# Two attention blocks in one program: the second mixer's lists, halves and engines rearranged

## The reference

```
first_block:  h = rms_norm(x); proj = h @ w_in
              MoBA heads (8) and forgetting heads (8), causal, 64 wide
              merged = gate0 * (o_a @ w_branch_moba) + gate1 * (o_b @ w_branch_fox)
              x = x + merged @ w_out;  x = x + ffn(rms_norm(x))        (conv, silu, product)
second_block: p = rmsnorm(x) @ w_in_2, split into hq, hf, hi, hg, sq, sk, sv, iq, ik, iw, mq
  hgrn2:  b = cumsum(log f);  A[t,s] = sum_k q[t,k] exp(b[t,k]-b[s,k]) k[s,k],  s <= t
          o = A @ v + carried state;   o = rmsnorm(o) * silu(g)       (4 heads, 128 wide)
  dsa:    score = sum_h iw[h] relu(iq[h] . ik); keep the 64 best keys of each query;
          softmax attention over them                                 (4 heads, 64 wide)
  mem:    softmax attention over 256 memory tokens                    (4 heads, 64 wide)
          x = x + concat(o_hg, o_sa, o_mem) @ w_out_2;  x = x + ffn(rmsnorm(x))
```

## Time and profile before

| | us |
|---|---|
| median of 3 runs | 847.26 |
| the profiled execution | 844.03 |
| its span | 842.2 |
| TensorE busy | 779.6 |
| VectorE busy | 543.4 |
| ScalarE busy | 469.4 |
| GpSimd busy | 86.4 |

### The profile page before, as it was taken

How to read it: one execution, slowest core, us unless ns; L and a number is a source line. 1 busy time by engine, 2 the same in 40 slices (tenths; PEclk the granted TensorE clock), 3 DMA queues, 4 the chain that set the end, 5 groups by cost and what they waited for, 6 DMA issues and landing times.

```text
span 842.2 us, 10581 instructions
## 1 busy us (share of the span) xinstructions
PE 779.6 (93%) x3775; PEld 637.5 (76%) x3775; DVE 543.4 (65%) x799; ACT 469.4 (56%) x724; POOL 86.4 (10%) x52
## 2 busy tenths in 40 slices
PE   7998889997999999999999798787869999999998
PEld 4886769985788888888887676565646888888886
DVE  4777765858368777775555569887673776665640
ACT  3756577783267877773545735352543776666430
POOL 0023000000000000000000156543231000000000
PEclk6999989999999999999999899897679999999999
DMA  8668353535067554565565433311001766554730
GB/s 276 211 194 267 104 142 130 184 109 174 25 222 235 179 179 162 197 200 175 161 215 167 125 100 101 100 50 51 25 26 51 236 224 199 181 176 176 247 134 25
DMA packets 70986, 129.14 MB, mean 153 GB/s; under 512 B 5576, under 2 KB 17824, under 8 KB 70817
## 3 DMA queue, kind: packets, MB, share of 16 engines
q1 hardware_dynamic: 70366, 125.91, 46.1%
q10 hardware_dynamic: 578, 2.69, 0.9%
HBM read 127.54 MB, written 1.05 MB: 153 GB/s over the span
## 4 chain that ended last, share of the span: by engine, by line
PE 74%; DVE 13%; ACT 8%; issue 2%; DMA 2%; POOL 1%; ACTq 0%; DVEq 0%; POOLq 0%
PE acc L486 21%; PE acc L488 21%; PE acc L487 21%; DVE b_wlo L1376 3%; PE banks L805 2%; ACT b_whi L939 1%; PE banks L818 1%; PE banks L629 1%; PE banks L503 1%; PE banks L549 1%; DVE b_ss L1447 1%; DVE b_qraw L1454 1%; DVE b_qraw L1461 1%; POOL b_rp L1929 1%; DVE b_spare L1777 1%
## 5 line engine op out<-in xcount | busy, mean ns | idle before, releaser
L1376 DVE TENSOR_TENSOR b_wlo<-b_raw,b_whi 128x1024 fp32r<-128x1024 f32 (+4 forms) x222 | 252.9, 1179 | 101.8 <-ACT b_whi L939 100.7
L939 ACT ACTIVATE b_whi<-b_raw 128x1024 fp32r<-128x1024 f32 (+4 forms) x244 | 235.2, 1002 | 77.8 <-PE acc L488 22.4
L486 PE MATMUL acc<-b_whi,b_hhi 128*128 128x512 f32 (+4 forms) x528 | 204.7, 388 | 8.4 <-DVE b_hlo L1750 4.7
L487 PE MATMUL acc<-b_whi,b_hlo 128*128 128x512 f32 (+4 forms) x528 | 198.2, 375 | 0.0
L488 PE MATMUL acc<-b_wlo,b_hhi 128*128 128x512 f32 (+4 forms) x528 | 198.0, 375 | 0.0
L486 PEld LDWEIGHTS acc<-b_whi,b_hhi 128*128 128x128 f32 x528 | 101.0, 191 | 28.6 <-DVE b_hlo L1750 5.2
L486 PE MATMUL acc<-b_whi,b_ohi 128*128 128x512 f32 (+1 forms) x272 | 107.4, 395 | 6.5 <-DVE b_wlo L1376 2.9
L487 PEld LDWEIGHTS acc<-b_whi,b_hlo 128*128 128x128 f32 x528 | 101.1, 191 | 16.0 <-issue 1.5
L488 PEld LDWEIGHTS acc<-b_wlo,b_hhi 128*128 128x128 f32 x528 | 100.8, 191 | 15.8
L487 PE MATMUL acc<-b_whi,b_olo 128*128 128x512 f32 (+1 forms) x272 | 104.5, 384 | 0.0
L488 PE MATMUL acc<-b_wlo,b_ohi 128*128 128x512 f32 (+1 forms) x272 | 104.4, 384 | 0.0
(11 more groups left out here) (247 smaller groups left out, 866.6 us busy)
## 6 DMA issues: line engine op xcount, KB each, us to landing
b_raw<-in_w_in SPq DMA_DIRECT2D x48, 512.0 KB, 4.6
b_raw<-in_w_ffn_up SPq DMA_DIRECT2D x40, 512.0 KB, 4.7
b_raw<-in_w_ffn_in SPq DMA_DIRECT2D x40, 512.0 KB, 4.6
b_raw<-in_w_ffn_down SPq DMA_DIRECT2D x22, 512.0 KB, 5.5
b_raw<-in_w_ffn_out SPq DMA_DIRECT2D x22, 512.0 KB, 4.4
b_raw<-in_w_out SPq DMA_DIRECT2D x16, 512.0 KB, 3.7
b_raw<-in_w_in SPq DMA_DIRECT2D x12, 412.0 KB, 4.3
b_raw<-in_w_in SPq DMA_DIRECT2D x8, 410.0 KB, 4.5
```

The lines of the kernel that those rows point to most:

```text
L486: nc.tensor.matmul(o, a, wh, start=first, stop=False)
L487: nc.tensor.matmul(o, b, wh, start=False, stop=False)
L939: A(whi[:, n % SPLIT, 0:c["nk"], 0:c["n"]], raw[:, n % RAW, 0:c["nk"], 0:c["n"]], ACT.Copy)\
L1376: V.tensor_tensor(wlo[:, n % SPLIT, 0:c["nk"], 0:c["n"]], raw[:, n % RAW, 0:c["nk"], 0:c["n"]], whi[:, n % SPLIT, 0:c["nk"], 0:c["n"]].bit ...
```

## The change

In the first mixer `("sums", "kb")` stands one place later, after `scores 1`. The merge is taken apart: VectorE alternates gating and L1750, the banks are waited for tile by tile, and `wo1_0` and `wo1_1` are streamed in turns. In the second mixer GpSimd has nothing left to do: its subtractions and `kd`, `kx` go to VectorE. The decay products take a rounded table and `logf` in two rounded parts. Pairs are computed only inside halves of 64 tokens (plus one 64 x 64 block across), so that one bank holds them; ScalarE places the result (`place`). Heads and index heads run two at a time. Group order and number of large products stay.

```diff
+            stream("wo1_0", "wo1_1")
+        elif n != "hf":
+            stream(n, part=1)            # second mixer's groups; the list names both parts together
-        FIRST = {0: [("sums", "qb")]}
+        FIRST = {0: [("sums", "qb")], 1: [("sums", "kb")]}
-        LAST = {0: [("sums", "kb")], 1: [("sums", "fg0")], ...
+        LAST = {1: [("sums", "fg0")], ...

+            merged_T(0); gemm("wo1_0", 0, norm="merged"); merged_T(1); gemm("wo1_1", 0)
+            gemm("wo1_0", 1, norm="merged")
+            gemm("wo1_1", 1, between=lambda: norm_T("ffn1", 0), between_at=1)

+            merge(0, 0)                  # VectorE: L1741 and L1746 of one tile
+            merge(0, 1)
+            merged_lo(0, 0)              # VectorE: L1750 of one tile
+            merge(1, 0)
+            merged_lo(0, 1)
+            merge(1, 1)
+            lo_to(groups["wo1_0"]["at"][1] + 1 * PART)
+            for t in range(T):
+                merged_lo(1, t)
+            norm("ffn1", "wo1_0", "wo1_1", ohi, olo, gain_at(2), PART, PART)

+        MIX2 = [... *parts("iqb")[2:], ("pairs", 0), ("place", 0), ("decay", 1), ("sums", "iqb"), ...
+                *parts("sqk")[:2], ("pairs", 4), ("place", 4), ("decay", 5), ("turn", "mq"), ("best", 0), ("best", 1),
+                ("scores", 8), *parts("sqk")[2:], ("divide", 8), ("pairs", 5), ("place", 5), ("probs", 8), ("decay", 6),
+                ("best", 2), ("pv", 8), ("best", 3), ("sums", "sqk"),
+                *parts("hg")[:2], ("hout", 2), ("pairs", 6), ("place", 6), ("scores", 9), ("divide", 9), ("probs", 9), ("decay", 7),
+                ("best", 4), ("best", 5), ("pv", 9), ("turn", "sqk"),
+                *parts("hg")[2:], ("pairs", 7), ("place", 7), ("hout", 3),
+                ("sums", "hg"), ("best", 6), ("best", 7), ("chosen", 0), ("hgrn norm", 0), ("log", "g"), ("scores", 10),
+                ("exp", "g"), ("gemm", "wo2_0", 0), ("gemm", "wo2_1", 0), ("divide", 10), ("hgrn norm", 1), ("probs", 10),
+                ("scores", 11), ("divide", 11), ("pv", 10), ("gain", 0), ("out", 0), ("out", 2), ("probs", 11),
+                ("gemm", "wo2_0", 1), ("pv", 11), ("gemm", "wo2_1", 1), ("gemm", "wo2_0", 2), ("gemm", "wo2_1", 2)]

# decay, TensorE
-                    full(nc.tensor.matmul(X[b][:, :], logf[...], hgc[:, c:c + 512], ...
+                    nc.tensor.matmul(X[b][:, :], lfhi[...], table, start=True, stop=False)      # rounded parts
+                    full(nc.tensor.matmul(X[b][:, :], lflo[...], table, start=False, stop=True), ...
# ScalarE, once each
+            done(A(hgr[:, C_HC:C_HC + 9 * P], hgc[:, C_HC:C_HC + 9 * P], ACT.Copy), "hgrn table", "0")
+                    done(A(lfhi[:, :, :], logf[:, :, :], ACT.Copy), "log f hi", "0")            # ahead of ("exp", "k")
# VectorE, once
+                    done(V.tensor_tensor(lflo[...], logf[...], lfhi[...].bitcast(F32), ALU.subtract), "log f split", "0")
# pairs, TensorE
+                for n in range(1, LEVELS + 1):
+                    for r in range(2):   # own: 64 rows of the bank and 64 tokens
+                        nc.tensor.matmul(X[2][own, (n - 1) * 64:n * 64], k, q, start=True, stop=True)
+                full(nc.tensor.matmul(X[2][0:64, LEVELS * 64:512], kd[:, 0, 0:64], qd[:, 0, 64:P], ...
# VectorE, unit u
+                V.tensor_tensor(qd[:, :, :], dec[...], q..., ALU.mult)
+                V.tensor_tensor(kd[:, :, :], dec[...], k..., ALU.mult)
+                (kx for even u, qx for odd u)
+                done(V.tensor_tensor(masked[:, :], X[2][:, 0:448], hgc[:, C_HM:C_HM + 448], ALU.mult), "pairs masked", ...
+                done(V.tensor_reduce(near[:, u % 2, :], masked (448 elements to 64), AX.X, ALU.add), "weights summed", ...
# ScalarE, unit u: "pairs" copies the 64 x 64 block across; "place", which the list puts before "decay u + 1":
+                    act.wait_ge(*at("weights summed", f"{n}"))
+                    A(AT[0:64, t, 0:64], near[0:64, t, :], ACT.Copy)
+                    done(A(AT[64:P, t, 64:P], near[64:P, t, :], ACT.Copy), "weights placed", f"{n}")
# ScalarE, "out": new wait
+                    act.wait_ge(*at("bank3 full", "probs 11"))
# VectorE, every ("gemm", ...) of the second mixer; GpSimd's loop is gone
-                    lo_to(min(part_end(n, *rest) + 3 * PART, MIX2_LOW[0] - 1))
+                    lo_to(part_end(n, *rest) + 3 * PART)
```

More of the change, by code:

```diff
@@ L462, in full, with gemm @@
                 done(ins, f"bank{bank} full", step, i)
[L464 removed]
+            def gemm(name, c=None, i=0, norm=None, between=None, between_at=0):
                 g = groups[name]
@@ L581, in pair_pv, with mixed_scores @@
                 full(mm, 2, f"pv {g}")
-            def attn_scores(j):
-                q, k, _, whole = head(j)
-                b = j % 2
-                claim(b, f"scores {j}")
-                for start, steps in ((16, ("sqk",)), (20, ("mq", "mk"))):
-                    if j == start:
+            def mixed_scores(g):
+                for i in range(2):
+                    claim(i, f"scores {g}")
+                for start, steps in ((10, ("sqk",)), (8, ("mq", "mk"))):
+                    if g == start:
@@ new lines, in mixed_divide @@
+            def mixed_divide(g):
+                two = slice(first_head(g), first_head(g) + 2)
+                for i in range(2):
+                    dve.wait_ge(*(at(f"bank{i} free", f"scores {g}") if whole(g) else at("exps ready", f"{g}")))
+                done(V.reciprocal(rc[:, two, :], sm[:, two, :]), "sum inverted", f"{g}")
+                dve.wait_ge(*at("sum inverted", f"{g}"))
+                for i in range(2):
+                    pr, j = pair_probs(g, i), first_head(g) + i
+                    for t, c0, n in pair_parts(g):
+                        ins = V.tensor_scalar(pr[:, c0:c0 + n], pr[:, c0:c0 + n], rc[:, j, t:t + 1], None, ALU.mult)
+                done(ins, "probs ready", f"{g}")
```

551 lines of the change are left out of this document (267 added, 284 removed).

## The result

The changed kernel took 840.75 us (median of 20 runs, 836.67 to 844.19), the kernel before 846.16 beside it (20 runs, 839.47 to 853.22): ratio 0.9938, 95% interval 0.9918 to 0.9958, so 5.3 us faster where 15 were forecast. The time lies at the upper end of the forecast's own range of 825 to 841, with about a third of the forecast gain. The profiled execution took 841.02 us, with a span of 839.2.

What follows compares the result with a forecast made beforehand. Second mixer taken as bound by ScalarE at its start, then TensorE, and VectorE's queue from 508 us; merge 4.1, keys 0 and second mixer 10.8 sum to 14.9 us off the 847.3 median: 832 us, range 825 to 841.

Steps and rivals of the forecast that it cites:

- Merge, 4.1 us forecast: End of the first mixer: shorter TensorE waits around the merged transposes gain 4.1 us net, bounds 6 gained to 1 lost.
- about 0.7 us may be lost on the next norm's second half: Norm behind the merge: interleaving leaves one chunk of cover for four VectorE instructions, so about 0.7 us lost.
- Keys, 0: First mixer, step moved past `scores 1`: only queue order changes, so 0, between 3 us gained and 2 lost.
- Second mixer, 10.8 forecast: Whole second mixer, 444 to 649 us: 10.8 us ahead at its end.
- Net 6.0 us: Second mixer, 533 to 604 us, VectorE's queue: 20.2 us of work gone less what is added, 6.0 us gained.
- 1.0 back: Second mixer, 604 to 649 us: 3.8 us saved against 4.8 of longer chain, so 1.0 us given back.
- The `place` waits beyond those there now 0.4: Second mixer, 533 to 604 us: extra waiting because `place` precedes the next unit's exponentials on ScalarE, 0.4 us added.
- 0.4 where two heads' exponentials (4 x 0.47) plus a rounding of 1.05 stand between maximum and subtraction: Second mixer, 533 to 604 us: ScalarE's work for a head pair makes VectorE wait, 0.4 us added.
- (b): Rival, slots from `sqk` to `wo2`: subtractions and `place` waits run serially, so 4 us slower, 851; chance 0.13.
- (a): Rival, second mixer: shorter VectorE-ScalarE chain halves gaps after 531 us and clock losses, 11 us more, 821; chance 0.19.
- (c): Rival, no change: freed VectorE time goes back into long gaps at low clock, only the merge stays, 845; chance 0.14.
- (d): Rival, second mixer's pairs: small tiles 0.5 us a unit slower, not 0.6 faster, 835; counted within the forecast's 0.54.

Runs made afterwards that it cites:

- b1: Kernel before with GpSimd's second-mixer work (22 subtractions, the decayed keys) moved to VectorE and nothing else of the change: 841.6 us.
- e1: Changed kernel with the end of its first mixer (merge, order of the two output groups, leads of the subtractions) as before: 841.9 us.
- e2: Changed kernel with the leads of the subtractions around the merge given back, the rest of the new merge kept: 835.7 us.
- c1: Changed kernel with e2, e4 and e5 joined, and ScalarE's copy of mq's transposes ahead of unit 4's placing: 826.9 us.
- c2: c1 with pair 9's scores one step earlier on all engines, its division and the rounds of the eight largest moved to suit on VectorE: 827.5 us.
- c3: c1 with more moves in VectorE's list alone (maxima, divisions and masks of several pairs and units put earlier): 816.1 us.
- e6: Changed kernel with the norm of kb back in its old place, one step earlier in all engines' lists: 842.5 us.
- e5: Changed kernel with ScalarE's list alone altered: for units 0 to 4 the next decay's exponentials ahead of the copies placing the present unit's weights: 837.3 us.
- e4: Changed kernel with the late second-mixer lists of VectorE and ScalarE reordered, TensorE's list and all operations unchanged: 832.9 us.
- e7: Changed kernel with the second mixer's subtractions back on GpSimd, the decayed keys left on VectorE: 845.9 us.
- e10: Changed kernel with each unit's mask product and sum over levels done twice on VectorE: time up by 14.2 us.

## Why the prediction was wrong

The direction was right, the size a third.

**Merge, 4.1 us forecast: mis-sized.** Measured 0.1 to 1.7 (44.9 against 45.0, 46.2, b1's 45.2 and e1's 46.6). The two waits fell as drawn (1.07 and 0.30; 0.9 and 0.6 were forecast). The step that failed is "about 0.7 us may be lost on the next norm's second half": 3.75 us of wait more, and behind it 14 products of 256 columns 0.21 us apart instead of 0.12. It counted VectorE's instructions between two products and not the loads that wait for its subtractions. With the leads kept the stage takes 40.0 to 40.7 us (e2, c1, c2, c3), 5 under before.

**Keys, 0: within its bounds.** The wait is 0.7 us shorter; e6 is 1.8 us above the changed kernel by the medians and 3 by the ratios, at the edge of what the intervals tell apart.

**Second mixer, 10.8 forecast: 1.5 to 5.2 measured**, by which profile of before one takes. The milestones came true as far as 525.73 us, where sqk's first products start (532.53 before; counted from the stage's start 9.0 us ahead, 9.7 forecast). At the first product of wo2_0, at 604.02 before and at 598.29 now, it is 8.0 us ahead (2.3 against the second profile of before), where 11.8 were forecast, and at the end 5.2 (1.5), where 10.8 were. Durations and busy times were right nearly throughout: `qd` and `kd` at 1.09, sums at 0.93 (0.88), masks 0.62, gain products 0.69, pairs 1.15 (1.3), decays 1.2 (0.92), VectorE 121.8 (123). What failed is the term for 533 to 604, "Net 6.0 us", which took TensorE no further ahead, and the one for 604 to 649, "1.0 back", with 2.7 back (0.8 by the second profile). In them it is the steps that translate work into time. "The `place` waits beyond those there now 0.4": unit 4's mask and placing hold decay 5's exponentials, and bank 0, for 5.20 us, and e5 gets 3.8 back. "0.4 where two heads' exponentials (4 x 0.47) plus a rounding of 1.05 stand between maximum and subtraction": with the heads in pairs the chain of maxima, exponentials and division stood behind subtractions, masks, norms and rounds of the eight largest in VectorE's queue, and the waits around it are of 10.4, 11.0 and 4.8 us (with that order changed e4 gets 8.0 back, c3 23). Gaps of the first two's size were foreseen ("three or four gaps of 8 to 10 us"), but "not fewer microseconds of idle than now" left open how many more. It was 17, and the prediction's own mark for its failure, 45 us in all, is passed with 53. b1 shows the error from the other side: what the stage gained is, as closely as these runs tell, the relief of GpSimd.

**The rivals.** (b) is false as a whole: its subtractions in VectorE's queue pay (e7), though two of them stand in the wait of 10.37 us. (a), shorter chains, needed the other order (c3 goes beyond its 821). (c) is nearest in its mechanism, freed time given back in long waits at the low clock, but the merge, which it kept, stayed away too. (d) is false: the small tiles take 0.65 us less a unit. "TensorEngine Tiling (Array Packing)" in the Trainium skill says that a product costs at least as much as one of 60 columns (Instruction Overhead) and that a change of mode drains the engine (Key Properties). The prediction read a price of 0 out of that, wrongly: these products have 64 columns, above that floor. The change of mode does show, and is small: 0.09 us more than the usual distance between starts on the way into the small products (0.24 from 485.82 to 486.06) and as much on the way out. The rule of "SBUF — State Buffer" in the Trainium skill (Who interferes with whom), that a VectorE instruction with two inputs in SBUF contends with a GpSimd one that reads SBUF, agrees with the traces: without GpSimd 1.09 and 1.22 us instead of 2.85 and 3.25.

**Open:** how the loss between b1 and the changed kernel divides among the pairs of heads, `place` and the later exponentials. By e10's price alone the 14 us of masks and sums that the change took off VectorE would have been some 12 us, an estimate, so by it the rest of the change cost about as much; no run takes that apart. That order alone is worth 23 us in the stage (c3) is shown; that the old list of single heads would have kept the saving isn't.

## What to carry to other kernels

Work taken off an engine is time only where that engine stands between a wait of the bound one and its end: double the work in question for one run, and read its price per microsecond (1.0 for VectorE's masks and sums here, 0.5 to 1.0 for TensorE's small products) before spending effort on it. When steps are merged or an engine takes over another's work, write each engine's queue anew: put what frees a bank or ends a chain first, and what only has to be done some time into the waits. And when subtractions or copies are moved, follow the loads that wait for their buffers, 20 us on.

## What was not expected of the hardware

The clock behind a short wait differs between executions of one and the same program; what decides isn't shown. In 18 profiles the stretch from `pv 7` to the merged transposes, with the same wait of 1.62 us in it, took 8.1 us in 7 and 9.6 to 9.7 in 11; the one from qb's transposes to the first scores, behind a wait of 1.6 to 3.9 us, 6.5 in 9 and 7.9 to 8.1 in 9. Both values of the first occur for before and for the changed kernel, both of the second for the changed one. A single pair of profiles of kernels that differ by under 4 us says little.

Beside GpSimd's subtractions it is the start that decides who pays. In e7 VectorE's product with the root of the mean began 0.36 us ahead of a GpSimd subtraction and took 1.23 us, its time alone; the two gain products behind it began inside GpSimd's instructions and took 2.7 each instead of 0.69:

```profile
563.04 1.23 DVE L1500 TENSOR_TENSOR b_tokA<-b_tokA,b_rs 128x1024 f32<-128x1024 f32 x1
564.30 5.46 DVE L1507 TENSOR_TENSOR b_tokA<-b_tokA,b_hgain 128x512 f32<-128x512 f32 x2
```

GpSimd's side, where the pair that met them took 5.81 us and a pair with VectorE idle 4.74:

```profile
563.40 5.81 POOL L2014 TENSOR_TENSOR b_wlo<-b_raw,b_whi 128x1024 fp32r<-128x1024 f32 x2 [10.43 <-ACT b_whi L963]
...
589.57 4.74 POOL L2014 TENSOR_TENSOR b_wlo<-b_raw,b_whi 128x1024 fp32r<-128x1024 f32 x2 [20.36 <-ACT b_whi L963]
```

The Trainium skill says in "SBUF — State Buffer" (Who interferes with whom) that the order of issue, not the shape of the operation, decides which of the two is blocked. The trace agrees. Short VectorE instructions are thus hurt most: in e7 a `kx` of 128x128, 0.28 us alone, took 2.48 where it began inside a GpSimd subtraction, and the four divisions ahead of `probs 8` took 3.28 us instead of 1.14, though each reads only one tensor in SBUF.
